# All attention steps among the transposed products, and each z projection after its branch's attention

## What is computed

```python
h = _rmsnorm(x, ln_g[l])
(qa, ka, va, za, qb, ckv, iq, ik, iw, zb, qc, kc, vc, zc, ga, gb, gc) = _split_cols(h @ w_in[l])
ya = _mixer_a(qa, ka, va, sink[l], t5_bias) * jax.nn.silu(za)
yb = _mixer_b(qb, ckv, iq, ik, iw, w_uk[l], w_uv[l], t5_bias) * jax.nn.silu(zb)
yc = _mixer_c(qc, kc, vc, c_rel_bias[l]) * jax.nn.silu(zc)
merged = (jax.nn.sigmoid(ga) * (ya @ w_pa[l]) + jax.nn.sigmoid(gb) * (yb @ w_pb[l])
          + jax.nn.sigmoid(gc) * (yc @ w_pc[l]))
x = x + merged @ w_o[l]
```

## Time and profile before

| | |
|---|---|
| median of 3 runs | 973.41 us (972.52 to 973.55) |
| profiled execution | 974.91 us, its span 972.9 us |
| PE busy | 961.7 us, 99% of the span |
| PEld busy | 812.4 us, 84% |
| DVE busy | 607.3 us, 62% |
| ACT busy | 472.7 us, 49% |
| POOL busy | 26.9 us, 3% |
| mean granted PE clock | 0.997 |
| chain that ended last | PE 93%, DMA 2%, DVE 2%, issue 1% |

### The profile page before, as it was taken

The page is one execution under the profiler, slowest core; times in us unless marked ns, Lnnn a source line. Parts: engine busy times, 40 slices in busy tenths (PEclk is TensorE's granted clock), DMA queues, the critical chain, the costliest instruction groups (busy, mean ns, idle before and its releaser), DMA issues.

```text
span 972.9 us, 13295 instructions
## 1 busy us (share of the span) xinstructions
PE 961.7 (99%) x5116; PEld 812.4 (84%) x5116; DVE 607.3 (62%) x1135; ACT 472.7 (49%) x786; POOL 26.9 (3%) x26
## 2 busy tenths in 40 slices
PE   9999999999999999999999999999999999999996
PEld 7788888888888888888888888788888888888885
DVE  7585755776675666586765655766655555555553
ACT  6564544555454554464453445544534443444442
POOL 0030000000000110010000000000000000000000
PEclk9999999999999999999999999999999999999998
DMA  8764765464553745564654745646455576555553
GB/s 338 276 193 131 236 192 186 158 226 164 203 210 119 261 169 185 184 218 147 220 204 136 265 156 170 216 154 218 169 189 184 190 302 219 190 182 186 175 178 124
DMA packets 54766, 190.34 MB, mean 196 GB/s; under 512 B 6192, under 2 KB 7088, under 8 KB 54064
## 3 DMA queue, kind: packets, MB, share of 16 engines
q1 hardware_dynamic: 54416, 189.23, 57.3%
q10 hardware_dynamic: 288, 0.27, 0.1%
HBM read 187.38 MB, written 2.10 MB: 195 GB/s over the span
## 4 chain that ended last, share of the span: by engine, by line
PE 93%; DMA 2%; DVE 2%; issue 1%; ACT 0%; SPq 0%; POOLq 0%; POOL 0%; DVEq 0%
PE bank L1016 24%; PE bank L1006 17%; PE bank L1007 17%; PE bank L1008 17%; PE bank L1019 12%; DMA raw<-in_w_s_dram 2%; PE bank L981 2%; PE bank L1052 2%; PE bank L1072 2%; DVE w_lo L626 1%; DVE hT L693 0%; ACT w_hi L444 0%; PE bank L1176 0%; DVE scores L658 0%; DVE scores L686 0%
## 5 line engine op out<-in xcount | busy, mean ns | idle before, releaser
L626 DVE TENSOR_TENSOR w_lo<-raw,w_hi 128x1024 fp32r<-128x1024 f32 (+2 forms) x326 | 387.9, 1214 | 173.7 <-ACT w_hi L444 172.7
L444 ACT ACTIVATE w_hi<-raw 128x1024 fp32r<-128x1024 f32 (+2 forms) x326 | 334.6, 1046 | 296.7 <-PE bank L1008 202.2
L1016 PE MATMUL bank<-hT,w_hi 128*128 128x512 f32 x976 | 306.2, 397 | 0.0
L1008 PE MATMUL bank<-w_hi,hT 128*128 128x512 f32 (+1 forms) x600 | 232.9, 388 | 0.0
L1019 PEld LDWEIGHTS bank<-hT,w_lo 128*128 128x128 f32 x976 | 181.1, 188 | 41.1
L1006 PE MATMUL bank<-w_hi,hT 128*128 128x512 f32 x504 | 197.1, 391 | 0.0
L1007 PE MATMUL bank<-w_lo,hT 128*128 128x512 f32 x504 | 196.1, 389 | 0.0
L1019 PE MATMUL bank<-hT,w_lo 128*128 128x256 f32 x976 | 190.9, 278 | 0.0
L1016 PEld LDWEIGHTS bank<-hT,w_hi 128*128 128x128 f32 x976 | 150.7, 189 | 3.9
L1008 PEld LDWEIGHTS bank<-w_hi,hT 128*128 128x128 f32 x600 | 112.6, 188 | 23.1
L1006 PE MATMUL bank<-w_hi,ybuf 128*128 128x512 f32 (+1 forms) x296 | 116.1, 392 | 1.4 <-DVE w_lo L626 0.9
(11 more groups left out here) (143 smaller groups left out, 511.6 us busy)
## 6 DMA issues: line engine op xcount, KB each, us to landing
raw<-in_w_s_dram SPq DMA_DIRECT2D x314, 512.0 KB, 4.4
bias_t<-in_bias_dram SPq DMA_DIRECT2D x24, 384.0 KB, 3.1
raw<-in_w_s_dram SPq DMA_DIRECT2D x6, 456.0 KB, 5.6
merged<-in_x_dram SPq DMA_DIRECT2D x2, 1024.0 KB, 11.1
raw<-in_w_s_dram SPq DMA_DIRECT2D x8, 256.0 KB, 3.3
big<-in_x_dram SPq DMA_DIRECT2D x1, 2048.0 KB, 9.6
out_dram<-big SPq DMA_DIRECT2D x8, 256.0 KB, 2.6
big<-in_x_t_dram SPq DMA_DIRECT2D x7, 256.0 KB, 5.9
```

Source lines behind the costliest of these rows:

```text
L444: nc.scalar.activation(halves(g)[0], raw[:, s, 0:n], ACT.Copy).then_inc(hi_ready, 1)
L626: nc.vector.tensor_tensor(low, raw[:, s, 0:n], high.bitcast(F32), ALU.subtract).then_inc(lo_ready, 1)
L1008: ins = mm(acc, xl, wh[:, e, :], start=False, stop=kt == n_kt - 1)
L1016: mm(bank[2 * (c % 2) + n][:, :], wh[:, e, n * P:(n + 1) * P], hl_t[:, kt, :, :], start=kt == 0, stop=False)
```

## The change

CHUNKS, slots() and `rounds` are changed so that all PE steps of attention stand between q1 and z(2,3). The 12 z quarters follow k directly, in one row. From q(1,0) on, a slot stands every five pieces for slots -1 to 6; from k on, an odd slot (values and scores) is followed by the even one (transposes) after five pieces and by the next odd one after two more, seven pieces for a group. The bias step, the exponentials and the normalization are each one piece closer to the scores.

The values no longer wait for silu(z): ACT copies them from PSUM into qT, four 128 x 128 copies a group (new), and DVE multiplies a z quarter's silu into qT at the end of that z chunk, two products of 128 x 256 (new), in place of DVE's four L643 products a group. `silu` shrinks to 2 x 256 columns. A new semaphore o_ready counts the copies; DVE's bias step waits for it. The split of y of branch b also waits for the end of P of branch b - 1.

```diff
-CHUNKS = ([("kvc", 0, 0), ("v", 0, 0), ("v", 0, 1), ("iq", 0, 0), ("ka", 0, 0)] + quarters("q", 0) + quarters("z", 0)
+CHUNKS = ([("kvc", 0, 0), ("v", 0, 0), ("v", 0, 1), ("iq", 0, 0), ("ka", 0, 0)] + quarters("q", 0)
...
-          + quarters("k", 0) + quarters("z", 1)
-          + branch(0) + quarters("z", 2) + branch(1) + branch(2) + quarters("o", 0))
+          + quarters("k", 0) + quarters("z", 0) + quarters("z", 1) + quarters("z", 2)
+          + branch(0) + branch(1) + branch(2) + quarters("o", 0))
...
-    yield -1, FIRST[AT["z", 0, 3]]
-    whole = [g for g in range(FIRST[AT["q", 1, 0]], END["k", 0, 3]) if KIND_OF[g] in "qk"]
-    for i in range(8):
-        yield i, whole[2 + 6 * i]
-    for b in range(2):
-        yield 8 * b + 8, FIRST[AT["z", b + 1, 0]] + 2
-        for k in range(7):
-            yield 8 * b + 9 + k, FIRST[AT["g", b, 0]] + 2 + 6 * k
+    for i in range(-1, 7):
+        yield i, FIRST[AT["q", 1, 0]] + 2 + 5 * (i + 1)
+    for i in range(7, 24):
+        yield i, FIRST[AT["k", 0, 0]] + 4 + 7 * ((i - 7) // 2) + 5 * (i % 2 == 0)
...
-                bias_at[SLOT_G[2 * (p // 2) - 3] + 5 + p % 2] = p
+                bias_at[SLOT_G[2 * (p // 2) - 3] + 6 + p % 2] = p
...
+                    elif q >= 0:
+                        sc.wait_ge(pv_ready, q + 1)
+                        sc.wait_ge(scored, min(q + 2, NPAIR // 2))
+                        for p in (2 * q, 2 * q + 1):
+                            for t in range(NT):
+                                nc.scalar.activation(qT[p // 8][:, p % 8, P * t:P * (t + 1)],
+                                                     bank[4 + 2 * (p % 2) + t][:, SROW:CH], ACT.Copy, scale=0.25
+                                                     ).then_inc(o_ready, 1)
...
-                    p = scored_at(g - 3 - e) + e
+                    p = scored_at(g - 2 - e) + e
...
-                    p = scored_at(g - 2 - e) + e
+                    p = scored_at(g - 1 - e) + e
...
+                        if p > 1:
+                            ve.wait_ge(o_ready, 2 * p - 2)
...
-                    p = scored_at(g - 4 - e) + e
+                    p = scored_at(g - 3 - e) + e
...
-                        silu[:, 2 * u + half, :], gate[:, half, 0:SEQ], 1.0, gate[:, half, SEQ:CH], ALU.add, ALU.mult)
+                        silu[:, half, :], gate[:, half, 0:SEQ], 1.0, gate[:, half, SEQ:CH], ALU.add, ALU.mult)
                 ins.then_inc(dve_evac, 1)
+                ve.wait_ge(dve_evac, dves_before(c + 1))
+                ve.wait_ge(o_ready, 4 * (4 * b + u + 1))
+                for half in range(2):
+                    m = 2 * u + half
+                    nc.vector.tensor_tensor(qT[b][:, m, :], qT[b][:, m, :], silu[:, half, :], ALU.mult
+                                            ).then_inc(y_ready, 1)
...
-            rounds = {("z", 0, 0): 0, ("z", 0, 1): 1, ("z", 0, 2): 2, ("z", 0, 3): 3, ("q", 1, 1): 4, ("q", 1, 3): 5,
-                      ("q", 2, 1): 6, ("q", 2, 3): 7}
+            rounds = {("q", b, u): 4 * b + u - 4 for b in (1, 2) for u in range(4)}
...
-                    wait(pe, y_ready, 4 * q)
+                    wait(pe, o_ready, 4 * q)
```

More of the change, by code:

```diff
@@ L140, in hybrid_trunk @@
         v_b = sb("v_b", [P, NT, BW])
-        silu = sb("silu", [P, 8, SEQ])
+        silu = sb("silu", [P, 2, SEQ])
         kT_a = sb("kT_a", [P, 2, SEQ])
@@ L282, in hybrid_trunk @@
         pv_ready = sem("pv_ready")
+        o_ready = sem("o_ready")
         y_ready = sem("y_ready")
@@ L492, in yT_split @@
             def yT_split(b, k):
-                sc.wait_ge(y_ready, 2 * (8 * b + 4 * k + 4))
+                sc.wait_ge(y_ready, 8 * b + 4 * k + 4)
+                if b > 0:
+                    sc.wait_ge(used, END["P", b - 1, 3])
                 nc.scalar.activation(y_hi[:, 4 * k:4 * k + 4, :], qT[b][:, 4 * k:4 * k + 4, :], ACT.Copy
@@ L770, in silu_chunk @@
                 _, b, u = CHUNKS[c]
-                wait(ve, y_ready, 2 * 8 * b)
                 for half in range(2):
```

## The result

The changed kernel takes 979.08 us (976.84 to 980.04), the one before 973.41 (972.52 to 973.69): 1.0052 times as long, interval 1.004 to 1.0063. It is slower by 5.7 us; 978.3 was forecast. The profiled execution took 980.04 us, its span 978.2.

What follows compares the result with a forecast made beforehand. PE was taken as full, so new cost could only be PE waiting for DVE and ACT. Waits of 6.05 us less gains of 1.1 gave net +4.9, 978.3 us against the median 973.41; range 974.2 to 981.8.

Steps and rivals of the forecast that it cites:

- PE is full: PE, 99% busy: only 0.87 us of waiting and 0.2 us of cheaper steps can be won, 1.1 us in all.
- group 8's wait: Before the change, group 8's transposes wait 0.87 us for DVE's normalization; the change can win this back.
- room from weight loads at 84%: Rival, PE has room: loads fit between transposed products, even half a step for eight moved ones gives 959.7 us; chance 0.02.
- Masks against the end of z(0,0): Group 6's window: POOL's masks stop DVE's two-input instructions; PE waits 0.45 for a low part, 3.15 at transposes, 3.6 us.
- the working by k: A z chunk ends k pieces after the scores; waits: k = 1 0.4 without masks, 2 0.15, 3 0.35, 0 and 4 none.
- Who comes first: Group 6, second mask against DVE's low part near C + 10.4: PE waits 3.15 us if mask first, 2.1 otherwise; 3.15 taken.
- C: In times such as C + 11.6: the end of a chunk on PE, here the z chunk in group 6's window.
- The small waits: PE waits of 0.55 at groups 0 and 1, 0.3 at 4, 0.15 at 7 and 11, 0.35 at 8, 0.4 at 10.
- The rival that wanted 0.5 us of slack in each chain: Cover holds: chains run 0.5 us shorter, small waits vanish (2.45 us), group 6 costs 2.5: 974.8 us; chance 0.22.
- ACT's copies: Copies of 128 x 128 from PSUM to qT: 0.27 us each, spaced by 0.2; bounds 0.2 and 0.5 spacing.
- DVE did not become the bound: Rival: with copies at 0.5 each, bias steps start 0.6 later, groups 1 to 11 lose 0.3 each: 981.5 to 983; chance 0.11.

Runs made afterwards that it cites:

- third experiment: The changed kernel with the transposes of groups 0 and 1 one piece later (slots 0 and 2): 977.61 us, 1.004 times the kernel before.
- the sixth: The changed kernel with DVE's new products at z chunk ends cut to one column instead of 256: 977.69 us, 1.0034 times the kernel before.
- fifth experiment: The changed kernel with POOL's mask also added to the eight pairs of branch C: 985.52 us, 1.0127 times the kernel before.
- seventh experiment: The changed kernel with bias loads four pieces later and transposes of groups 0 and 1 one piece later: 972.66 us, 0.9992 times the kernel before.

## Why the prediction was right, and where it was right by luck

**PE is full.** Right. The steps cost the same in their new place, and apart from group 8's wait only the remainder of 0.4 was won. The rule of the Trainium skill (Perfetto Trace Analysis, "Identifying the Most-Contended Engine") that would read room from weight loads at 84% got no support: 83% after, and none of the eight moved steps became cheap.

**Masks against the end of z(0,0).** Right in mechanism and place, and in size nearly (3.26 us of waits for 3.6), and shown from three sides: without masks, with the masks moved, and with the chunk's end moved the wait goes; with masks for C it comes back, largest where the chunk ends one piece behind the scores, absent at group 9, as the working by k had it. The Trainium skill's rule (SBUF — State Buffer, "Who interferes with whom") agrees with both orders: a mask stops a two-input DVE instruction from its start (2.77, 2.90), and such an instruction stops the mask (2.77 for 1.85).

**Who comes first.** This step failed. I let 3.15 or 2.1 us hang on whether mask or low part is first, and there is no working for the 2.1. With the low part first, its end at C + 11.6 and a normalization of 1.42 would have made PE only 1.4 us late if nothing stopped that normalization. But its first instruction is the denominator L678, with two SBUF inputs, and that stood for 1.77 us. Measured: 2.76 (twice) and 2.79 with the low part first, 2.69, 2.82 and 2.85 with the mask first. DVE loses about one mask in either order: 1.62 us at the denominator, 1.55 to 1.68 at the low part. What was 3.15 was oversized by 0.3 to 0.46, like nearly all my chains.

Nor would one SBUF input have kept the normalization safe. In the window of group 4 of the changed kernel (DVE, then the mask beside it):

```profile
291.88 0.18 DVE L681 RECIPROCAL r_denom<-denom 128x4 f32<-128x4 f32 x1
292.09 2.34 DVE L686 TENSOR_SCALAR scores<-scores,r_denom 128x256 f32<-128x256 f32 x4
...
291.78 1.85 POOL L424 TENSOR_TENSOR bias_t<-bias_t,chosen 128x768 f32<-128x768 f32 x1
```

The four L686 take 1.01 together elsewhere. Here they take 2.34, all of the loss in the first (1.69 instead of 0.35), which ends 0.15 after the mask. The reciprocal beside the same mask kept its 0.18.

**The small waits.** All there, in the right groups, and all too large but the low part's (0.50 for 0.45): by 0.09 and 0.12 at 0 and 1, 0.26 at 4, 0.12 each at 7 and 11, 0.13 at 8, 0.23 at 10, so 1.1 us too much in all. At group 8 a part of that is rounding: C + 5.85 against C + 5.58 is 0.27, not 0.35. The rival that wanted 0.5 us of slack in each chain had the sign right. The third experiment confirms that 0 and 1 are of another origin than 6; the sixth, that the new product costs 0.2 and 0.13 at 8 and 10, which I had inside those sums.

**The clock.** Not in the sum at all. Its 1.68 us more than fill the 1.41 us by which the waits were oversized, and that is luck. Had the clock not fallen, the kernel would have taken about 977.4 us (979.08 - 1.68), still in the range and still slower. The total is closer than its terms.

**ACT's copies.** Bounds 0.2 to 0.5 for their spacing, 0.2 taken, and the row says so:

```profile
331.81 0.79 ACT L458 ACTIVATE big<-bank 128x128 f32<-128x128 f32 x4 [4.71 <-PE bank L1076]
```

Four take 0.79 together, and DVE did not become the bound.

## What to carry to other kernels

When attention-like side work is packed closer to its deadline, list for each window what else the serving engine must do in it, and look above all for an engine that shares a resource with it: a 1.85 us POOL instruction at a place with no slack cost PE 2.8 us (4.9 with all that the masks brought on), and the same one four pieces later cost next to nothing. Move the intruder (here the load that triggers it) before undoing the change. And price a wait of PE with what may come behind it, a lower clock.

## What the runs showed of the hardware that I had not expected

- **A wait of under 3 us can halve PE's clock for a while, and does not always.** Waits of 2.76 (twice), 2.79, 2.82 and 2.85 us at group 6, in four kernels, were followed by a stretch at 1.2 GHz; after 2.69 us at group 10 and after 1.79 us at group 8 (fifth experiment) the granted clock stayed 1.00. In the changed kernel it cost 1.68 us, over half as much again as the wait itself. Where the line lies, these runs don't tell.
- **The size of an instruction says nothing about how long it stands.** A 128 x 4 addition of 0.15 us took 1.77 beside a mask, as long as the work of the mask that was left.
- **POOL is stopped as well.** A mask of 1.85 us alone took 2.77 with a low part at its start.
- **One SBUF input is no protection, an input from PSUM was.** L686 reads one tensor and a column of factors, all in SBUF, and took 1.67 to 1.88 us instead of 0.35 or 0.29 beside a mask, in six of the nine profiles with masks. The copies L643, which read PSUM, kept their 0.55 us beside the mask at 348.65 of the seventh experiment.
